# A two-block transformer kernel: buffer placement, norm factors from token-major squares, and a transposed result

## The reference

```python
def rmsnorm(x, g):
    y = x * lax.rsqrt(jnp.mean(x * x, axis=-1, keepdims=True) + 1e-6)
    return y * g
...
def memory_attention(q, mem, mem_g, w_mem_kv):
    mn = rmsnorm(mem, mem_g)
    kv = (mn @ w_mem_kv).reshape(b, m, 2, MEM_HEADS, HEAD_DIM)
...
def pool_layer(x, mem, norm_g, w_in, ...):
    h = rmsnorm(x, norm_g)
    proj = h @ w_in
    ...
    return x + jnp.concatenate([y_pool, y_mem], axis=-1) @ w_out
...
x = pool_layer(x, mem, ...); x = nsa_layer(x, mem, ...)
x = rmsnorm(x, final_g)
... # attention of a third kind, then a gated feed-forward of width 5632
return rmsnorm(x, final_norm)          # (1, 256, 2048)
```

## Time and profile before

| | us |
|---|---|
| three runs: median, lowest, highest | 2088.69, 2088.55, 2091.04 |
| the profiled execution | 2088.68 |
| its span | 2086.9 |
| busy: PE, DVE, ACT, POOL | 2051.0, 1482.5, 1021.6, 483.1 |
| first matmul begins | 7.83 |
| last weight matmul ends | 2072.08 |
| DMA traffic, queue q1 | 368 MB, 55.2% of 16 engines |

### The profile page before, as it was taken

The page is one execution under the profiler, slowest core; times in us unless marked ns, Lnnn a source line. Parts: engine busy times, 40 slices in busy tenths (PEclk is TensorE's granted clock), DMA queues, the critical chain, the costliest instruction groups (busy, mean ns, idle before and its releaser), DMA issues.

```text
span 2086.9 us, 29262 instructions
## 1 busy us (share of the span) xinstructions
PE 2051.0 (98%) x11470; PEld 1754.1 (84%) x11470; DVE 1482.5 (71%) x2056; ACT 1021.6 (49%) x1508; POOL 483.1 (23%) x442
## 2 busy tenths in 40 slices
PE   7999999999999999999999999999999999999997
PEld 6788888888788888888878888888888888888886
DVE  8866778789777556876656668777776557777765
ACT  5445444466533554654455555444444344454443
POOL 8305553300000344330212225211010000110122
PEclk9999999999999999999999999999999999999998
DMA  7555566566654333555444445555556665555664
GB/s 251 171 185 156 178 188 197 184 207 221 221 179 160 119 104 122 183 198 191 162 153 150 144 149 186 188 182 188 185 187 181 186 193 184 189 183 184 184 186 131
DMA packets 104089, 370.03 MB, mean 177 GB/s; under 512 B 11632, under 2 KB 12944, under 8 KB 103824
## 3 DMA queue, kind: packets, MB, share of 16 engines
q1 hardware_dynamic: 103952, 368.16, 55.2%
HBM read 366.02 MB, written 2.10 MB: 176 GB/s over the span
## 4 chain that ended last, share of the span: by engine, by line
PE 92%; DVE 6%; ACT 1%; issue 0%; POOL 0%; DMA 0%; DVEq 0%; ACTq 0%
PE psg L531 51%; PE psg L533 24%; DVE s_w L1622 2%; PE psg L578 2%; PE psg L580 2%; PE psg L579 2%; PE psg L530 2%; PE pst L531 1%; PE pst L617 1%; DVE s_rh L1640 1%; PE pst L533 1%; DVE s_ry L1640 1%; PE pss L793 1%; PE pso L813 0%; ACT s_w L1084 0%
## 5 line engine op out<-in xcount | busy, mean ns | idle before, releaser
L1622 DVE TENSOR_TENSOR s_w<-s_stage,s_w 128x1024 fp32r<-128x1024 f32 (+2 forms) x699 | 871.1, 1247 | 368.8 <-ACT s_w L1084 365.6
L1084 ACT ACTIVATE s_w<-s_stage 128x1024 fp32r<-128x1024 f32 (+2 forms) x699 | 728.3, 1043 | 789.2 <-PE psg L531 423.7
L531 PE MATMUL psg<-s_ry,s_w 128*128 128x512 f32 x2656 | 939.0, 401 | 3.7 <-DVE s_mv L1689 2.5
L533 PE MATMUL psg<-s_ry,s_w 128*128 128x256 f32 x2486 | 698.7, 281 | 0.0
L531 PEld LDWEIGHTS psg<-s_ry,s_w 128*128 128x128 f32 x2656 | 490.9, 189 | 116.3 <-issue 4.1
L533 PEld LDWEIGHTS psg<-s_ry,s_w 128*128 128x128 f32 x2486 | 470.8, 189 | 7.3
L531 PE MATMUL psg<-s_rh,s_w 128*128 128x512 f32 x1280 | 458.6, 404 | 11.9 <-DVE s_rh L1640 9.5
L533 PE MATMUL psg<-s_rh,s_w 128*128 128x256 f32 x1180 | 332.4, 282 | 0.0
L531 PEld LDWEIGHTS psg<-s_rh,s_w 128*128 128x128 f32 x1280 | 237.9, 189 | 65.2 <-issue 8.1
L531 PE MATMUL psg<-s_hid,s_w 128*128 128x512 f32 x704 | 245.9, 399 | 0.0
L533 PEld LDWEIGHTS psg<-s_rh,s_w 128*128 128x128 f32 x1180 | 224.6, 190 | 3.7
(11 more groups left out here) (388 smaller groups left out, 2224.8 us busy)
## 6 DMA issues: line engine op xcount, KB each, us to landing
s_stage<-in_wo SPq DMA_DIRECT2D x96, 512.0 KB, 3.5
s_stage<-in_wg SPq DMA_DIRECT2D x88, 512.0 KB, 3.5
s_stage<-in_wu SPq DMA_DIRECT2D x88, 512.0 KB, 3.6
s_stage<-in_ain SPq DMA_DIRECT2D x64, 512.0 KB, 3.6
s_stage<-in_wd SPq DMA_DIRECT2D x64, 448.0 KB, 3.4
s_stage<-in_wkv SPq DMA_DIRECT2D x32, 512.0 KB, 4.0
s_stage<-in_wd SPq DMA_DIRECT2D x32, 512.0 KB, 3.5
s_stage<-in_bq SPq DMA_DIRECT2D x24, 512.0 KB, 3.5
```

The source lines that it names most:

```text
L531: m = e.matmul(o, M.WH[:, r, ws], xx, start=begin, stop=end)
L533: m = e.matmul(o[:, T:2 * T], M.WL[:, r, ws], xh, start=False, stop=False)
L1084: e.activation(M.weights(c, 0, n), M.staged(c, n), ACT.Copy).then_inc(S["wh"], 1)
L1622: e.tensor_tensor(M.weights(c, 1, n), M.staged(c, n), M.weights(c, 0, n), ALU.subtract).then_inc(S["wl"], 1)
```

## The change

**Placement.** The small buffers are allocated first; then `s_pad` fills up to a multiple of 1024 bytes, and all large ones follow, each a multiple of 1024 long. `s_stage` now begins at 24576, `s_w` at 40960, `s_x` at 65536, `s_ry` at 95232, `s_rh` and `s_hid` at 128000.

**Start.** Unit 0 is loaded in two halves by ACT's DMA queue, cast and subtracted in halves behind slabs 0 and 2, and PE waits for each half only. SP loads first the 16 gain columns that slab work needs, then mem in smaller pieces. The rest of the table comes later, x after unit 10.

**Input norms.** mem and x are loaded a second time, tokens on the partition (`s_tm`, 2 MB each). ACT squares them in 128x512 pieces with a sum along the row; DVE adds the four sums, ACT and DVE make the factors as 128x2 columns, DVE multiplies them into the identity matrix, and one matmul with ones gives the row form, which ACT copies to `s_rb`. POOL's squares of mem and x are gone.

**End.** PE transposes the sixteen slabs (32 transposes of 128x128) into eight PSUM banks. The norm gives columns only. ACT evicts the first 128 tokens, DVE the second, four pieces of 512 features each, scaled by the token's factor, and SP stores each (eight transfers of 256 KB) in token-major form.

```diff
-        self.ST = fix("stage", [128, NS, UW])
-        self.W = fix("w", [128, NR, 2, UW], F32R)
...
+        self.PAD = fix("pad", [128, -((nc.sbuf_base + 31) // 32 * 32) % 1024 // 4])
+        self.ST = fix("stage", [128, NS, UW])
+        self.W = fix("w", [128, NR, 2, UW], F32R)
...
+def result(P, M, t, q):
+    i, last = NORM["fin"] % 2, P.bank[("wd", 1), KT - 1][1]
+    banks = (M.PSS[:, 0, :], M.PSS[:, 1, :], M.PST[:, 0, :], M.PST[:, 1, :], M.PSO[1 - i][:, :], M.PSG[1 - last][:, :],
+             M.PSG[last][:, :], M.PSO[i][:, :])
+    return banks[2 * q + t]
... tensor_program
+            if c == 0:
+                w.wait_ge("wh" if kk >= 4 else "wh_a", 1)
             m = e.matmul(o, M.WH[:, r, ws], xx, start=begin, stop=end)
+            if c == 0:
+                w.wait_ge("wl" if kk >= 4 else "wl_a", 1)
...
+    def token_rows(n, ticks):
+        for _ in range(ticks):
+            yield
+        i = NORM[n]
+        vacant(("o", i % 2))
+        w.wait_ge("nr_dg", i + 1)
+        for t in range(2):
+            m = e.matmul(M.PSO[i % 2][:, t * 128:t * 128 + 128], ones, M.NW[:, t * 128:t * 128 + 128], start=True, stop=True)
+        m.then_inc(S["nr_mm"], 1)
...
     w.wait_ge("sql", 15)
+    sums(M.ACC[1], True)
+    turn(0, 0)
+    turn(0, 1)
     w.wait_ge("sq15", 1)
-    norm_rows("fin", [(ones, M.ACC[1][:, :]), (ones, M.YT[0][:, :])])
-    side.drain()
+    sums(M.YT[0], False).then_inc(S["nr_mm"], 1)
+    for q in (1, 2):
+        turn(q, 0)
+        turn(q, 1)
+    w.wait_ge(*P.out[("wd", 1), KT - 1])
+    turn(3, 0)
+    w.wait_ge("nr_dve", 3 * NORM["fin"] + 1)
+    turn(3, 1)
... scalar_program
+    def token_norm(n, rc, ticks):
+        i = NORM[n]
+        for _ in range(ticks):
+            yield
+        for t in range(2):
+            w.wait_ge(f"l_tm{i}", 16)
+            for q in range(4):
+                src = M.TM[:, t, 512 * q:512 * q + 512]
+                x = e.activation(src, src, ACT.Square, accum_out=M.CSQ[:, i, t, q:q + 1])
+            x.then_inc(S["sqt"], 1)
+            yield
...
+    for half, name in enumerate(("st_a", "st0")):
+        ws = slice(512 * half, 512 * half + 512)
+        e.dma_start(M.ST[:, 0, ws], P.units[0][0][:, ws]).then_inc(S[name], 16)
     tables()
... vector_program, end
-    norm_rows("fin", 1, 0)
     side.drain()
+    norm_cols("fin", 1, 0)
     normed("fin")
-    for n, (a, b) in enumerate(((0, 1), (1, 3), (3, 6), (6, 9), (9, 11))):
-        w.wait_ge("xg", b)
-        for j in range(a, b):
-            x = e.tensor_tensor(M.X[:, j, :], M.X[:, j, :], M.RB[1][:, :], ALU.mult)
-        x.then_inc(S["fin_dve"], 1)
+    for q in range(4):
+        w.wait_ge("turned", 2 * q + 2)
+        e.tensor_scalar(M.OT[:, 1, 512 * q:512 * q + 512], result(P, M, 1, q), M.RC[1][:, 1:2], None, ALU.mult).then_inc(S["fin_dve"], 1)
... pool_program
-    for j in range(8):
-        w.wait_ge(("l_mem0", "l_mem1", "l_mem2", "l_mem2")[j // 2], 16)
-        square(M.ACC[0][:, :], j, M.MEM[:, j, :], "sqm")
-    side.start(mem_rest())
     ticks(16)
-    for j in range(KT):
-        w.wait_ge(f"l_x{j // 4}", 16)
-        square(M.ACC[1][:, :], j, M.X[:, j, :], "sqx")
```

More of the change, by code:

```diff
@@ L947, in tensor_program @@
     H0 = H
-    w.wait_ge("eps", 5)
-    side.start(mem_norm())
+    side.start(token_rows("mem_c", 15))
     group([("mk", 0, j) for j in range(4)], H, ready("m0"))
@@ L954, in tensor_program @@
     side.start(lam())
+    side.start(token_rows("x_c", 13))
     group([("mk", 1, j) for j in range(4)], Y, ready("m1"))
     pair(("mv", 1), Y, ready("m1"))
-    w.wait_ge("sqx", KT)
-    norm_rows("x", [(ones, M.ACC[1][:, :])])
     for j in range(4):
@@ L1135, in silu, with first @@
         e.activation(M.ET[i % 2][:, :], M.ZT[i % 2][:, :], ACT.Tanh).then_inc(S["z_t"], 1)
+    def first(half):
+        done[0], ws = 1, slice(512 * half, 512 * half + 512)
+        w.wait_ge(("st_a", "st0")[half], 16)
+        e.activation(M.WH[:, 0, ws], M.ST[:, 0, ws], ACT.Copy).then_inc(S[("wh_a", "wh")[half]], 1)
     def mem_rest():
@@ L1729, in mem1, with first, token_norm @@
             yield
+    def first(half):
+        done[0], ws = 1, slice(512 * half, 512 * half + 512)
+        w.wait_ge(("wh_a", "wh")[half], 1)
+        e.tensor_tensor(M.WL[:, 0, ws], M.ST[:, 0, ws], M.WH[:, 0, ws], ALU.subtract).then_inc(S[("wl_a", "wl")[half]], 1)
+    def token_norm(n, rc, ticks):
+        i = NORM[n]
+        for _ in range(ticks):
+            yield
+        w.wait_ge("sqt", 2 * i + 2)
+        e.tensor_reduce(M.CSM[:, i, :], M.CSQ[:, i, :, :], AX.X, ALU.add).then_inc(S["csm"], 1)
+        yield
+        yield
+        refine(n, M.RC[rc][:, :], M.CSM[:, i, :], M.CW[:, 0:2], EPV[0] * D)
+        normed(n)
+        w.wait_ge("l_con", 16)
+        if i:
+            w.wait_ge("nr_mm", i)
+        for t in range(2):
+            x = e.tensor_scalar(M.NW[:, t * 128:t * 128 + 128], M.con("ident", 128), M.RC[rc][:, t:t + 1], None, ALU.mult)
+        x.then_inc(S["nr_dg"], 1)
     def mem_norm():
-        for _ in range(9):
+        yield from token_norm("mem_c", 0, 11)
+        for _ in range(5):
             yield
-        norm_rows("mem", 0, 0)
-        yield
-        norm_cols("mem_c", 0, 0)
-        yield
-        normed("mem")
+        w.wait_ge("nr_rb", 1)
         for j in range(4):
@@ L2115, in hidden @@
         e.tensor_tensor(M.HH[j % 2][:, :], M.UU[j % 2][:, :], cv[:, :], ALU.mult).then_inc(S["ff_h"], 1)
-    split()
     for j in range(8):
         low(M.RH, j, M.MEM[:, j, :], M.vec("mg0", j), "m0")
-        if j in (3, 7):
-            split()
+        if j in (0, 2):
+            first(j // 2)
+    split()
+    split()
     side.start(mem_rest())
@@ L2132, in vector_program @@
     side.start(setup())
+    side.start(token_norm("x_c", 1, 9))
     nxt(4)
```

171 lines of the change are left out of this document (94 added, 77 removed).

## The result

Four runs of the changed kernel gave 2073.46 to 2074.52 us, median 2073.67, beside 2088.62 (2088.22 to 2091.04) of the kernel before: 0.9927 of the time, 95% interval 0.991 to 0.9944, a gain of 14.95 us where 16.9 were forecast. The profiled execution took 2074.52 us, span 2072.7.

What follows compares the result with a forecast made beforehand. VectorE, slow while POOL squares, was taken to bound the start up to 66 us, TensorE the middle. Start 13.2 plus end 3.7, placement nothing, made 16.9 us: 2088.7 to 2071.8 us, range 2065 to 2079.

## What to carry to other kernels

When DVE is slow by a constant factor in one stretch, look at what POOL reads there before anything else; moving the reads to another engine, even in another layout and with twice the loads, gave 12 of the 15 us here. Where PE streams without a gap and still takes longer than its columns, try the distance between the weights' buffer and the activations' buffer in steps of 32 bytes: it is a one-line edit, and its effect (16 us here, either kernel) shows in the distance of matmul starts in one profile. A block of tiny matmuls between large ones costs more than its own time if the clock falls in it; spread it.

## What the runs showed of the hardware

- The same pair of matmuls, 512 and 256 columns, starts every 352.4, 351.2 or 347.6 ns by nothing but the distance between weights and activations (0, 64, 32 bytes within 256); with roles exchanged (value tiles, where the weights stream), distance 0 is the fast one, 228.5 against 233.3 ns. The Trainium skill, "SBUF — State Buffer", Who interferes with whom, knows only the port of GpSimd and VectorE as a place of contention; the measurement shows another effect of addresses, on PE alone.
- The clock fell within a block of 48 matmul records of 15 columns (PE busy throughout by the timeline), in each of eleven profiles that had them in one block, and in none of three that had them in four. The earlier in the block it fell, the longer it stayed down: 10.2, 6.8 or 3.4 us.
- 32 transposes of 128x128 float32 ran at full clock behind the last weight matmuls, eight of them in 1.07 us.
